# The opening of a five-layer forward pass on one NeuronCore, built in another order

## The reference, cut to what matters

```python
def rms_norm(x, g):
    y = xf * lax.rsqrt(jnp.mean(xf * xf, axis=-1, keepdims=True) + NORM_EPS)
    return (y * g.astype(jnp.float32)).astype(x.dtype)
...
hn = rms_norm(x, norm_gains[i, 0])
m = diff_attention(hn, a_w_in[inst], ...)      # i = 0: qkv = hn @ w_in
x = x + rms_norm(m, norm_gains[i, 1])
f = swiglu(rms_norm(x, norm_gains[i, 2]), ffn_w_gate[i], ffn_w_up[i], ffn_w_down[i])
x = x + rms_norm(f, norm_gains[i, 3])
```

## Time and profile before

| what | value |
|---|---|
| median of three runs | 1369.65 us |
| the profiled execution's own time | 1370.82 us |
| its span, first to last instruction | 1369.1 us |
| PE busy | 1346.4 us, 98% of the span |
| DVE busy | 1020.4 us, 75% |
| ACT busy | 790.7 us, 58% |
| chain that ended last | PE 83%, DVE 13%, ACT 3%, DMA 1% |

### The profile page before, as it was taken

How to read it: one execution, slowest core, us unless ns; L and a number is a source line. 1 busy time by engine, 2 the same in 40 slices (tenths; PEclk the granted TensorE clock), 3 DMA queues, 4 the chain that set the end, 5 groups by cost and what they waited for, 6 DMA issues and landing times.

```text
span 1369.1 us, 20597 instructions
## 1 busy us (share of the span) xinstructions
PE 1346.4 (98%) x6811; PEld 1105.8 (81%) x6811; DVE 1020.4 (75%) x1930; ACT 790.7 (58%) x1546; POOL 177.1 (13%) x323
## 2 busy tenths in 40 slices
PE   7999999999999999999999999999999999999998
PEld 6888888889987888889888888888888888887657
DVE  6978666669666766669766665699887777889976
ACT  6676555456555655458656544566665455675344
POOL 4100000000111000002000000001049992000000
PEclk9999999999999999999999999999999999999999
DMA  8534766675433777783336777744457666553132
GB/s 283 165 124 132 237 215 222 215 242 188 158 106 113 241 215 222 231 244 109 123 106 210 222 231 229 231 165 158 126 178 229 227 216 214 171 184 123 62 123 93
DMA packets 180309, 249.24 MB, mean 182 GB/s; under 512 B 10392, under 2 KB 124640, under 8 KB 180240
## 3 DMA queue, kind: packets, MB, share of 16 engines
q1 hardware_dynamic: 152352, 224.05, 50.4%
q10 hardware_dynamic: 25920, 18.89, 4.6%
q0 software_dynamic: 1968, 5.43, 1.4%
HBM read 237.84 MB, written 10.49 MB: 181 GB/s over the span
## 4 chain that ended last, share of the span: by engine, by line
PE 83%; DVE 13%; ACT 3%; issue 1%; DMA 1%; ACTq 0%; SPq 0%; DVEq 0%
PE ps L2112 21%; PE ps L2114 21%; PE ps L2113 21%; DVE w_rest L1382 3%; PE ps L2118 3%; PE ps L2126 3%; PE ps L2122 3%; ACT w_head L830 1%; PE ps L2142 1%; PE ps L2448 1%; PE ps L2933 1%; PE ps L2934 1%; PE ps L2935 1%; PE ps L2965 1%; DVE x L1445 1%
## 5 line engine op out<-in xcount | busy, mean ns | idle before, releaser
L2112 PE MATMUL ps<-w_head,xt_head 128*128 128x512 f32 (+1 forms) x1152 | 448.0, 389 | 3.3 <-DVE w_rest L1382 2.9
L2114 PE MATMUL ps<-w_head,xt_rest 128*128 128x512 f32 (+1 forms) x1152 | 441.5, 383 | 0.0
L2113 PE MATMUL ps<-w_rest,xt_head 128*128 128x512 f32 (+1 forms) x1152 | 441.0, 383 | 0.0
L830 ACT ACTIVATE w_head<-w_raw,gain_t 128x512 fp32r<-128x512 f32 (+1 forms) x596 | 375.1, 699 | 84.2 <-PE ps L2114 24.1
L1382 DVE SCALAR_TENSOR_TENSOR w_rest<-w_raw,gain_t,w_head 128x512 fp32r<-128x512 f32 (+1 forms) x596 | 417.2, 764 | 5.5 <-ACT w_head L830 4.7
L2112 PEld LDWEIGHTS ps<-w_head,xt_head 128*128 128x128 f32 x1152 | 217.1, 188 | 48.3 <-issue 6.4
L2114 PEld LDWEIGHTS ps<-w_head,xt_rest 128*128 128x128 f32 x1152 | 217.1, 188 | 43.0
L2113 PEld LDWEIGHTS ps<-w_rest,xt_head 128*128 128x128 f32 x1152 | 217.4, 189 | 39.7
L830 ACT ACTIVATE w_head<-w_raw 128x1024 fp32r<-128x1024 f32 x124 | 124.6, 1053 | 81.6 <-PE ps L2114 76.9
L1380 DVE TENSOR_TENSOR w_rest<-w_raw,w_head 128x1024 fp32r<-128x1024 f32 x124 | 146.8, 1222 | 7.1 <-ACT w_head L830 6.7
L1990 DVE SCALAR_TENSOR_TENSOR hid<-ps,rstd_x,gate_s 128x256 f32<-128x256 f32 x88 | 38.5, 479 | 119.9 <-ACT gate_s L1126 119.9
(11 more groups left out here) (502 smaller groups left out, 1700.7 us busy)
## 6 DMA issues: line engine op xcount, KB each, us to landing
w_raw<-in_ffn_w_gate_dram SPq DMA_DIRECT2D x88, 512.0 KB, 4.3
w_raw<-in_ffn_w_up_dram SPq DMA_DIRECT2D x88, 512.0 KB, 5.9
w_raw<-in_ffn_w_down_dram SPq DMA_DIRECT2D x88, 512.0 KB, 6.2
w_raw<-in_a_w_in_dram SPq DMA_DIRECT2D x48, 512.0 KB, 4.8
w_raw<-in_b_w_in_dram SPq DMA_DIRECT2D x24, 512.0 KB, 4.7
w_raw<-in_w_in_dram SPq DMA_DIRECT2D x24, 512.0 KB, 4.6
hid_way<-q_t ACTq DMA_DIRECT2D x36, 256.0 KB, 2.0
k_t<-hid_way ACTq DMA_DIRECT2D x144, 64.0 KB, 5.1
```

The costliest lines, as they stand in the source:

```text
L830: ins = act.activation(w_head[:, s, w], raw(u)[:, w], ACT.Copy, scale=1.0 if by is None else by)
L2112: pe.matmul(out_, hd, wh, start=first, stop=False)
L2113: pe.matmul(out_, hd, wr, start=False, stop=False)
L2114: return pe.matmul(out_, rt, wh, start=False, stop=last)
```

## The change

- Two queues: the gain rows are fetched by ACT's queue, no longer by SP's; `x` comes in four quarters, placed between the halves of unit 0 and behind it. The first half of unit 0 has a semaphore of its own (`first_in`). POOL's small transfers wait until the second half of unit 0 is there.
- The gain of the first layer is multiplied into `x` while it is rounded (`first_heads` on ACT, `first_rest` on DVE, four tiles of 128 x 128 each, since each has its own gain column). The 12 weight units of the first projection are then split without a gain, in pieces of 1024 columns (unit 0: of 512).
- PE's `opening` replaces `entry`: per group first all products of two heads, then those with the rest of `x`, then those with the rest of the weights. It starts with ten products of a cleared tile (`filled`), in lots of 5, 2 and 3; their results are not used.
- On DVE the angles come after `rest(2)`; the late rows are turned and copied at step 3 and after the second chunk, and sine and cosine are made after `head(3)`.

```diff
     for li, kind in enumerate(LAYERS):
-        out += [(4 * li, k, kt) for ch in in_chunks(kind) for _, _, k, kt in ch]
+        out += [(4 * li if li else None, k, kt) for ch in in_chunks(kind) for _, _, k, kt in ch]
         out += [(None, k, kt) for ch in out_chunks() for _, _, k, kt in ch]
...
             row, k0, kt = WEIGHTS[u]
+            if u == 0:
+                return [(slice(512 * t, 512 * t + 512), None, 1) for t in range(4)]
             if row is None:
...
             first = CONSTS["inv_freq"][1]
             sp.dma_start(const[:, 0:first], a["constants"][:, 0:first]).then_inc(ident_in, 16)
-            sp.dma_start(gain_rows, a["norm_gains"].rearrange("l r d -> (l r) d")).then_inc(gain_rows_in, 16)
-            sp.dma_start(x[:, 0, :], a["x"][0, 0:P, :]).then_inc(x_in[0], 16)
+
+            def x_load(g):
+
+                m, w = g // 2, cols_of(g % 2)
+                sp.dma_start(x[:, m, w], a["x"][0, P * m:P * m + P, w]).then_inc(x_in[g], 16)
+
+            x_load(0)
 
             def load(u, more, dst1, src1, dst2, src2):
...
                 there = gate_raw_in if u == FIRST_GATE else raw_in[u % RING]
-                sp.dma_start(dst1, src1).then_inc(there, 16)
+                sp.dma_start(dst1, src1).then_inc(there if u else first_in, 16)
+                if u == 0:
+                    x_load(2)
                 sp.dma_start(dst2, src2).then_inc(there, 16)
 
...
-                                sp.dma_start(x[:, 1, :], a["x"][0, P:2 * P, :]).then_inc(x_in[1], 16)
+                                x_load(1)
+                                x_load(3)
                             if u == 3:
                                 sp.dma_start(const[:, first:N_CONST], a["constants"][:, first:N_CONST]).then_inc(const_in, 16)
...
+            pool.wait_ge(raw_in[0], 16)
             pool.dma_start(pos_i[:, :], a["positions"][0].rearrange("(m p) -> p m", p=P), allow_slow_non_contiguous=True).then_inc(pos_in, 16)
...
                     if s >= 4:
                         exp(s - 4)
+                    if first and s == 0:
+                        rotary()
                     if first and s == 2:
...
 
-            entry(True, norm=False, groups=(0, 1))
+            def first_heads(g):
+
+                n["xt"] += 1
+                act.wait_ge(xt_ready, n["xt"])
+                for t in range(4):
+                    k = 4 * (g % 2) + t
+                    last = act.activation(xt_head[:, k, P * (g // 2):P * (g // 2) + P], ps[:, 6 + g // 2, P * t:P * t + P], ACT.Copy,
+                                          scale=gain_t[:, k, 0:1])
+                last.then_inc(xt_head_done, 1)
+
+            act.dma_start(gain_rows, a["norm_gains"].rearrange("l r d -> (l r) d")).then_inc(gain_rows_in, 16)
             act.wait_ge(gain_there, 1)
-            head(0)
+            first_heads(0)
+            head(0, some=(0, 2))
+            first_heads(2)
+            head(0, some=(2, 4))
+            first_heads(1)
             head(1)
-            rotary()
-            entry(True, norm=False, groups=(2,))
+            first_heads(3)
             head(2)
-            entry(True, groups=(3,))
+            square_of_x(0)
+            square_of_x(1)
             u = 0
...
                 for s in range(12):
+                    if li == 0 and s == 1:
+                        dve.wait_ge(trig_done, 1)
+                        dve.wait_ge(const_in, 16)
                     if s in (1, 2, 5, 7):
                         chunk_out(s // 2)
+                    if li == 0 and s == 2:
+                        late_copies()
                     if s >= 4:
...
 
+            def first_rest(g):
+
+                n["xt"] += 1
+                dve.wait_ge(xt_head_done, n["xt"])
+                for t in range(4):
+                    k, w = 4 * (g % 2) + t, slice(P * (g // 2), P * (g // 2) + P)
+                    last = dve.scalar_tensor_tensor(xt_rest[:, k, w], ps[:, 6 + g // 2, P * t:P * t + P], gain_t[:, k, 0:1],
+                                                    xt_head[:, k, w].bitcast(F32), ALU.mult, ALU.subtract)
+                last.then_inc(xt_rest_done, 1)
+
+            dve.memset(scr_v[:, 0, 0:2 * P], 0.0).then_inc(fill_there, 1)
             dve.wait_ge(gain_turned, 1)
             dve.tensor_copy(gain_t[:, :, 0:MIX_ROW], ps[:, 5, 0:KT * MIX_ROW].rearrange("p (k r) -> p k r", k=KT)).then_inc(gain_there, 1)
             dve.wait_ge(gain_there, 1)
-            xt_rest_of(0, True)
-            xt_rest_of(1, True)
-            rest(0)
+            first_rest(0)
+            rest(0, some=(0, 2))
+            first_rest(2)
+            rest(0, some=(2, 4))
+            first_rest(1)
+            rest(1)
+            first_rest(3)
+            rest(2)
 
             dve.wait_ge(ident_in, 16)
             dve.wait_ge(pos_in, 16)
...
-            rest(1)
...
-            xt_rest_of(2, True)
-            rest(2)
-            xt_rest_of(3, True)
             norm_of_x()
+
+            def late_copies():
+
+                R = KT * (G_ROWS - MIX_ROW)
+                dve.wait_ge(late_turned, 1)
+                dve.tensor_copy(gain_t[:, :, MIX_ROW:G_ROWS], ps[:, 5, 0:R].rearrange("p (k r) -> p k r", k=KT))
+                dve.tensor_copy(s5_par_t[:, :], ps[:, 5, R:R + PAR]).then_inc(late_there, 1)
 
 
...
                     first_half_turned()
 
-            def entry(u, waits, by_half, second=1, between=lambda: None):
-
-
-
-                def transposes(g):
-                    pe.wait_ge(*waits[g])
+            def opening():
+
+                def filled(count):
+                    for _ in range(count):
+                        pe.matmul(ps[:, 4, 0:P], scr_v[:, 0, 0:P], scr_v[:, 0, P:2 * P], start=True, stop=True)
+
+                def turned(g):
+                    pe.wait_ge(x_in[g], 16)
                     if n["xt"] >= 2:
                         pe.wait_ge(xt_rest_done, n["xt"] - 1)
...
+                    for t in range(4):
+                        k, m = 4 * (g % 2) + t, g // 2
+                        last = pe.transpose(ps[:, 6 + m, P * t:P * t + P], x[:, m, P * k:P * k + P], ident)
                     last.then_inc(xt_ready, 1)
                     n["xt"] += 1
 
-                def products(g):
...
-                base = n["xt"]
-                transposes(0)
-                transposes(1)
-                products(0)
-                between()
-                transposes(2)
-                products(1)
-                transposes(3)
-                products(2)
-                products(3)
+                def heads(g, tiles=range(4)):
+                    half, m = g % 2, g // 2
+                    for t in tiles:
+                        pe.wait_ge(head_done, 4 * half + t + 1)
+                        by_heads(ps[:, m, :], XT, 4 * half + t, m, half, 512 * t, 512, half + t == 0)
+
+                def x_rests(g, tiles=range(4)):
+                    half, m = g % 2, g // 2
+                    for t in tiles:
+                        by_x_rest(ps[:, m, :], XT, 4 * half + t, m, half, 512 * t, 512)
+
+                def w_rests(g, tiles=range(4)):
+                    half, m = g % 2, g // 2
+                    for t in tiles:
+                        pe.wait_ge(rest_done, 4 * half + t + 1)
+                        last = by_w_rest(ps[:, m, :], XT, 4 * half + t, m, half, 512 * t, 512, half == 1 and t == 3)
+                    return last
+
+                pe.wait_ge(fill_there, 1)
+                filled(5)
+                gains_turned()
+                filled(2)
+                turned(0)
+                filled(3)
+                pe.wait_ge(xt_head_done, 1)
+                heads(0, (0, 1))
+                pe.wait_ge(xt_rest_done, 1)
+                x_rests(0, (0, 1))
+                turned(2)
+                w_rests(0, (0, 1))
+                heads(0, (2, 3))
+                x_rests(0, (2, 3))
+                w_rests(0, (2, 3))
+                turned(1)
+                pe.wait_ge(xt_head_done, 2)
+                heads(2)
+                pe.wait_ge(xt_rest_done, 2)
+                x_rests(2)
+                w_rests(2).then_inc(unit_used, 1)
+                turned(3)
+                pe.wait_ge(xt_head_done, 3)
+                heads(1)
+                pe.wait_ge(xt_rest_done, 3)
+                x_rests(1)
+                w_rests(1)
+                pe.wait_ge(xt_head_done, 4)
+                heads(3)
+                pe.wait_ge(xt_rest_done, 4)
+                x_rests(3)
+                w_rests(3).then_inc(unit_used, 1)
 
...
                     pe.wait_ge(rope_added, rope_ + M * (D_CHUNK[i] + 1))
-                    if i == 7:
+                    if i == 2:
                         pe.wait_ge(late_there, 1)
...
                 for s in range(2, 12):
                     unit(s)
+                    if first and s == 3:
+                        late_rows_turned()
                     for i in D_SLOT.get(s, ()):
                         turn_group(i)
...
```

(5 more changed lines are left out.)

39 lines of the change are left out of this document (12 added, 27 removed).

## The result

| | before | changed | ratio, 95% interval |
|---|---|---|---|
| first measurement, 6 and 6 runs | 1369.52 us | 1378.59 us | 1.0064 [1.0053, 1.0075] |
| second measurement, 11 and 6 runs | 1369.23 us | 1375.70 us | 1.0046 [1.0033, 1.0059] |
| profiled execution of the first | 1370.82 | 1375.78 (span 1374.0) | |

The change costs 6 to 9 us. The forecast was slower, with 1372.5 us and a range that ended at 1375.5; both measured medians lie above it.

The account below looks back on a forecast made before the run. Behind the opening PE and DVE were taken as both nearly full. DVE's lateness of 1.9 at the second `mix` plus 1.0 for slow clock gave +2.9, 1372.5 us against the median; own range 1371 to 1374, whole range 1365.5 to 1375.5.

Parts of the forecast that it names:

- First product at 10.1: PE's opening: first real product at 10.1 us, 1.3 earlier than before, with cleared products priced at 0.22 each.
- The table load on the path: ACT's function table load, 1.28 us, stands behind the wait for turned x and delays the first heads; no drain counted.
- The chain of hand-offs: PE, ACT and DVE pass groups in turn, each waiting: from heads at 9.5 to unit 1 split at 21.5 us.
- one slow hand-off: Only the first of two transposes in the chain runs at the lower clock: +1.0 us.
- DVE's queue behind it: DVE's work from unit 1's split to the second chunk sums to 18.4 us, so that chunk starts 2.0 late.
- POOL's share: POOL's casts and subtraction slow DVE beside them: 1.6 us, falling on unit 2 and the angles.
- The wait at unit 3: PE waits for DVE at units 3 and 4: idle 1 to 2 us around 30 to 40 us.
- The late `mix`: DVE makes the second pair's `mix` 1.9 late, plus 1.0 for slow clock; PE idles about 1.5 near 63 us.
- The missing gain gives nothing: Cheaper unit splits on DVE (2.3 instead of 2.73) give nothing for two pairs of later units: per pair +0.1 us.
- The clock at the opening: First products run at 1.2 GHz, 0.43 apart; the clock is up by about 16 us.
- The faster one: Rival: PE alone bounds the kernel, its opening ending at 22.4 us: -4.1, 1365.5 us; chance 0.22.
- Worse than the sum: Rival: the table load's drain counts, or the clock stays low through group 1: +4.5 to +6, 1375 us; chance 0.08.

Follow-up runs that it names:

- angles_back: The changed kernel with DVE's angles moved back between the rests of units 0 and 1: 1373.19 us, ratio 1.0025 to the kernel before.
- masks_early: The changed kernel with POOL's two casts and subtraction placed ahead of its wait for unit 0's last product: 1373.48 us, ratio 1.0031 to the kernel before.
- wait_filled: The changed kernel with five unused products of the identity put into PE's wait at unit 3: 1376.70 us, ratio 1.0050 to the kernel before.
- gain_in_x_alone: The kernel before with only the first layer's gain multiplied into x and the function table loaded first: 1371.56 us, ratio 1.0008.
- cleared_ahead_mended: four_mended plus earlier turning of groups on PE, POOL's small transfers issued at once, and seven cleared products where PE idles: 1367.37 us, ratio 0.9983.
- four_mended: The changed kernel without cleared products, with table loaded first, angles in DVE's early pause and POOL's masks cast early: 1370.22 us, ratio 1.0004.

## Why the prediction was wrong in size

- **First product at 10.1: 2.1 too early.** The first step that failed is the price of a cleared product, 0.22 from the row of the transposes. It was 0.49, two records each: a transpose of 128 columns fills one record, a product of the same size in plain float32 two. Seven of them ahead of the turned group cost 1.9 more. "FP8 and Floating Point Precision" in the Trainium skill (TensorE Precision Notes) gives four passes for a true FP32 product. By that, 4 x 128 columns at 1.2 GHz would be 0.43, an estimate from that page; the rows show 0.49, which is near it, but they show two records and not passes. I had it on the path, but looked up its price in a row of another kind of instruction.
- **The table load on the path: right.** 1.28 at 9.11, with the next activation at 10.40. The drain of 1.38 us in the Trainium skill (ScalarE: Activation LUTs, What ACT_TABLE_LOAD costs) is not in the trace: 0.01 us lie between, and taking the load away gave 1.26.
- **The chain of hand-offs: right.** From the first heads (forecast 9.5, measured 11.54) to unit 1's split (21.5, measured 24.27) I had 12.0, and 13.0 with the one slow hand-off that the value of the forecast includes; it took 12.7. The same holds for PE's opening: 25.1, 1.0 for that hand-off and 2.1 for the first product give 28.2, measured 28.19. (The working in brackets beside the 25.1 is that of the kernel before, 26.8; the 25.1 follows from group 2's last product at 19.2 and 24 products more.) Later experiments showed that the chain isn't what bounds a mended kernel; in the changed one it was.
- **DVE's queue behind it: 18.4 forecast, 19.4 measured** (24.27 to 43.67). The step that was mis-sized is POOL's share, taken as 1.6 from the earlier trace rows. It was up to 2.9: 0.95 on the split, 1.7 on the angles, which took 4.2 instead of 2.5, and 0.25 on the steps of `rstd`; the four rests were 0.25 shorter than forecast. I had priced it on splits alone; short operations suffer more, the cast sixfold. "GPSIMD Engine Reference" in the Trainium skill (1. Specifications) tells of contention with DVE instructions that have two SBUF inputs or run in a two-port mode. The split fits the first. Of what mode the small rows run in no trace tells anything.
- **The wait at unit 3: forecast as 1 to 2, measured 2.4. The pace behind it: missed.** I had reckoned the clock at the start only, and took a wait as costing its own length. Here 2.40 of waiting brought 1.80 more on PE. Of that 0.6 at most reached the end, as DVE was late too.
- **The late `mix`: the path was right, its terms too small.** I carried DVE's lateness, 1.9 and 1.0 for the slow hand-off, to the second `mix`. There DVE is 5.53 late. At its second chunk it is 5.77 late (37.90, 43.67) where I had 3.0: 2.04 more from the first group, 0.27 less in the chain, 1.00 more in the queue. This path alone makes 5.8 of the 6.39 at the marker (6.39 less the 0.6 that PE could have started earlier). No wait stands at the second `mix`, against my sign for it, since PE had lost a little more on its own by then, at unit 3, in the low clock behind it and in the late rows. The wait appears (0.58) in angles_back, masks_early and wait_filled, where DVE is late and PE has no low clock at unit 3. So the sum has to be made up twice, for PE at unit 3 and for DVE at `mix`, and the larger counts.
- **The missing gain gives nothing: right.** gain_in_x_alone shows it, and the row at the first reciprocal of the changed kernel is as forecast, DVE idle 0.65 behind a piece of 1024:

```profile
53.94 1.23 DVE L1416 TENSOR_TENSOR w_rest<-w_raw,w_head 128x1024 fp32r<-128x1024 f32 x1
55.81 0.18 DVE L1894 RECIPROCAL rcp<-den 128x4 f32<-128x4 f32 x1 [0.65 <-ACT pr L1026]
```

- **The clock at the opening: right, with luck.** Up at 16.88 to 17.7, against "until about 16". In other kernels whose opening has the same instructions on PE it was up at 12.4 (wait_filled) or at 22 (angles_back).
- **The rivals.** The faster one fails as forecast: unit 1 was split at 24.3, not by 19. Another order reaches its 22.4: in cleared_ahead_mended PE starts unit 2 at 21.54, though its time, 1367.4, stays above the rival's 1365.5. "Worse than the sum" (1375) came nearest in its time and had the smallest chance; its two reasons (a drain, a low clock in the opening) were not the ones.

So the direction and the path held, and the sizes failed: the cleared products (1.9 more), POOL's share (1.3 more, 1.0 in the whole queue), and the low clock behind a wait, which was at nothing (0.6 at the end). PE's own starts add up to 1.38 + 2.40 + 1.80 + 0.77 = 6.35, against 6.39 at the marker. The medians are 6.5 and 9.1 apart; the difference between these two is not in any trace.

## What to carry to other kernels

Price an added instruction by a row of its own kind, and put filler work only where nothing stands behind it: moving five cleared products ahead of a wait brought the first product 2.3 us forward. When two engines become late, make up the sum for each, at each place where one waits for the other, and let the larger count. Here mending PE's low clock alone gave nothing, as DVE was nearly as late. Work of a helper engine that may lie anywhere should lie where the other one idles; here it ran beside the only queue that was late, and moving 4 us of it was worth 2.5 to 3.5. Look again after each move: in four_mended the same work had come to lie beside another split on the path.
